# An encoder trunk's opening: transposes of x tiles in one row, or one tile at a time between the key/value products

## The reference

```python
proj = x @ w_in          # x (1, 512, 1024), w_in (1024, 512 + 2*128 + 2*512)
q, k, v, u = jnp.split(proj, [ATTN_WIDTH, ATTN_WIDTH + KV_WIDTH, ATTN_WIDTH + 2 * KV_WIDTH], axis=-1)
...
q = apply_rope(rms_norm(q, q_norm_g), cos, sin)
k = apply_rope(rms_norm(k, k_norm_g), cos, sin)
attn = block_attention(q, k, v)
conv = conformer_conv(u, dw_w, dw_b, conv_norm_g, conv_norm_b)
return jnp.concatenate([attn, conv], axis=-1) @ w_out
```

## Time and profile before

| what | value |
|---|---|
| time, median of 3 runs | 1415.85 us (1415.79 to 1416.1) |
| time of the profiled execution | 1417.29 us |
| span in the profile, first to last instruction | 1415.5 us |
| PE busy | 1389.9 us, 98% of the span |
| DVE, ACT, POOL busy | 656.0, 453.2, 117.6 us |
| mean granted clock of TensorE | 0.998 of full speed |

### The profile page before, as it was taken

One profiled execution on the slowest core, in us unless ns is written; L12 is line 12 of the kernel. 1 busy time (PEld: TensorE's weight loads), 2 busy tenths in 40 slices (PEclk: granted clock), 3 DMA queues, 4 the chain that ended last, 5 costly groups with the idle time before them and its releaser, 6 DMA issues.

```text
span 1415.5 us, 16267 instructions
## 1 busy us (share of the span) xinstructions
PE 1389.9 (98%) x6577; PEld 1157.4 (82%) x6577; DVE 656.0 (46%) x829; ACT 453.2 (32%) x601; POOL 117.6 (8%) x115
## 2 busy tenths in 40 slices
PE   7998999999999999999999999999999999999997
PEld 7876778988888888898888888888898888888886
DVE  5689966533333311266455554554264333332215
ACT  3448844332223211134232323333133232222111
POOL 5001012100000000060202020000030000000000
PEclk9999999999999999999999999999999999999999
DMA  6210002322332332222221212131323322333221
GB/s 215 73 49 31 30 31 62 118 89 90 100 106 89 119 111 97 89 75 90 86 93 59 89 59 89 60 119 62 112 65 97 111 89 89 112 107 108 90 89 60
DMA packets 84014, 124.14 MB, mean 88 GB/s; under 512 B 2688, under 2 KB 61312, under 8 KB 83968
## 3 DMA queue, kind: packets, MB, share of 16 engines
q1 hardware_dynamic: 83968, 123.49, 26.7%
HBM read 121.39 MB, written 2.10 MB: 87 GB/s over the span
## 4 chain that ended last, share of the span: by engine, by line
PE 91%; DVE 5%; ACT 1%; POOL 1%; issue 1%; DMA 0%; DVEq 0%; POOLq 0%; SPq 0%; ACTq 0%
PE ps L1228 23%; PE ps L1230 23%; PE ps L1229 23%; PE ps L1303 19%; DVE acc L868 1%; PE ps L1241 1%; POOL w_lo L375 1%; DVE w_lo L375 1%; DVE probT_lo L990 1%; ACT w_hi L371 1%; DVE neg_max L968 1%; PE ps L1444 0%; PE ps L1578 0%; DMA x_tok<-in_x 0%; DVE x_tok L1051 0%
## 5 line engine op out<-in xcount | busy, mean ns | idle before, releaser
L375 DVE TENSOR_TENSOR w_lo<-raw,w_hi 128x2048 fp32r<-128x2048 f32 x103 | 236.3, 2294 | 479.4 <-ACT w_hi L371 479.3
L1228 PE MATMUL ps<-xT_hi,w_hi 128*128 128x512 f32 (+1 forms) x992 | 366.7, 370 | 0.5 <-POOL w_lo L375 0.5
L1230 PE MATMUL ps<-xT_hi,w_lo 128*128 128x512 f32 (+1 forms) x992 | 365.6, 369 | 0.0
L1229 PE MATMUL ps<-xT_lo,w_hi 128*128 128x512 f32 (+1 forms) x992 | 365.5, 368 | 0.0
L371 ACT ACTIVATE w_hi<-raw 128x2048 fp32r<-128x2048 f32 x109 | 208.4, 1912 | 413.8 <-PE ps L1230 237.9
L1228 PEld LDWEIGHTS ps<-xT_hi,w_hi 128*128 128x128 f32 x992 | 187.0, 188 | 32.4 <-POOL w_lo L375 1.1
L1229 PEld LDWEIGHTS ps<-xT_lo,w_hi 128*128 128x128 f32 x992 | 187.0, 189 | 31.1
L1230 PEld LDWEIGHTS ps<-xT_hi,w_lo 128*128 128x128 f32 x992 | 187.0, 188 | 30.9
L1228 PE MATMUL ps<-w_hi,xT_hi 128*128 128x512 f32 (+1 forms) x320 | 121.3, 379 | 0.0
L1230 PE MATMUL ps<-w_hi,xT_lo 128*128 128x512 f32 (+1 forms) x320 | 121.1, 379 | 0.0
L1229 PE MATMUL ps<-w_lo,xT_hi 128*128 128x512 f32 (+1 forms) x320 | 121.1, 378 | 0.0
(11 more groups left out here) (161 smaller groups left out, 1611.3 us busy)
## 6 DMA issues: line engine op xcount, KB each, us to landing
raw<-in_l_w_in SPq DMA_DIRECT2D x31, 1024.0 KB, 5.2
raw<-in_l_ffn_w_gate SPq DMA_DIRECT2D x22, 1024.0 KB, 5.3
raw<-in_l_ffn_w_up SPq DMA_DIRECT2D x22, 1024.0 KB, 5.3
raw<-in_l_ffn_w_down SPq DMA_DIRECT2D x22, 1024.0 KB, 4.8
raw<-in_l_w_out SPq DMA_DIRECT2D x12, 1024.0 KB, 4.9
x_tok<-in_x SPq DMA_DIRECT2D x4, 512.0 KB, 7.5
out<-x_tok SPq DMA_DIRECT2D x8, 256.0 KB, 2.2
ln_gb<-in_l_ln_mix_g SPq DMA_DIRECT2D x2, 512.0 KB, 5.0
```

The costliest lines, as they stand in the source:

```text
L375: eng.tensor_tensor(w_lo[ch.s][:], raw[ch.s][:], f32(w_hi[ch.s][:]), ALU.subtract)\
L1228: nc.tensor.matmul(dst, a[0], b[0], start=start, stop=False)
L1229: nc.tensor.matmul(dst, a[0], b[1], start=False, stop=False)
L1230: return nc.tensor.matmul(dst, a[1], b[0], start=False, stop=stop)
```

## The change

The transposes of tile 0 still come first. Those of tile t + 1 are now issued inside `token_tiles`, ahead of the products of tile t, where the wait for the `xT_lo` of tile t also stands. The instructions are the same, in another order on PE; no other engine's text changes.

```diff
-            for t in range(TT):
-                turn_when_landed(t)
-            token_tiles([Chunk(C_KV)], SIDE_B, KD, 256, lambda t: pe.wait_ge(xT_lo_made, 2 * t + 2))
+            turn_when_landed(0)
+
+            def next_tile(t):
+
+                if t < TT - 1:
+                    turn_when_landed(t + 1)
+                pe.wait_ge(xT_lo_made, 2 * t + 2)
+
+            token_tiles([Chunk(C_KV)], SIDE_B, KD, 256, next_tile)
```

## The result

The changed kernel takes 1420.1 us in the median of 14 runs (1417.79 to 1420.7), the kernel before 1416.57 in 14 runs beside them (one of these took 6268.94 us; without it the median is 1416.54). The ratio is 1.002, with a 95% interval of 1.0014 to 1.0027: slower, by about 0.25% or 3.5 us, where 0.6 us was forecast and 1418.2 was the end of the range. The runs lie in two groups: 5 at 1417.8 to 1418.3 and 9 at 1420.0 to 1420.7, none between. The profiled run is one of the upper group, 1420.13 us with a span of 1418.3.

The account below looks back on a forecast made before the run. PE was taken to bound the kernel, busy 1389.9 of 1415.5 us. A new 1.19 us idle, less 0.58 because it falls where PE is slow, gave +0.6 us: 1416.45 us, own range 1416.2 to 1417.0, full range 1415.7 to 1418.2.

Parts of the forecast that it names:

- PE has no idle time to fill: From the first transpose at 7.8 us to 80 us, PE has no idle time that interleaving could fill.
- the new wait: After tile 0's transposes, at 9.53 us, PE waits for the first w_lo until 10.72: 1.19 us lost.
- The free change between transposes and products: Key/value products: switching between transposes and products costs nothing; at most 0.05 us allowed for each of six changes.
- the cover of chunk 1 and of the key work: Later splits and DVE's key work still finish before PE wants them; chunk 1's w_lo with 0.5 to 0.7 us left.
- d = 0: Opening: PE's rise to the high clock level stays at 13.7 us, so the 1.19 us idle costs 0.61 us.
- d/2: Opening: cost added to 0.61 us if the clock rise comes d later, since PE then does half the work.
- rival (a): Opening: the interrupted work delays the clock rise up to 16.6 us, costing up to +2.06 us, 1417.9; 24 in 100.
- my 2.06 us: Opening: upper sum, 0.61 + 1.45, if the low-level time is spent anew from 10.72 and PE rises at 16.6.
- the rest of the kernel is moved by PE's delay alone: After the opening all engines follow PE, and nothing there absorbs the 0.6 us delay.
- (b): Opening: PE stays at the low clock through the interleaving; up to +7.5 us, 1423.3; 5 in 100.
- (c): Opening: without a profiler the weights land earlier against x, so no idle time and 1415.85 us; 7 in 100.
- (c2): Opening: only products raise the clock, so the rise comes 1.75 us earlier, paying back 0.87: 1415.6; 2 in 100.

Follow-up runs that it names:

- e1: Changed kernel, but tiles 0 and 1 transposed ahead of the wait for the first w_lo, the others between the products; 1416.51 us, ratio 1.0.
- e2: Kernel before, all transposes in one row, with only the wait for the first w_lo put behind tile 0's transposes; 1418.27 us, ratio 1.0015.
- e9: Changed kernel with 14 unread identity transposes put into PE's 1.8 us pause before the last channel tile's first tap; 1418.24 us.
- e7: Kernel before, unchanged, run and profiled again; 1416.58 us in 8 runs.
- e3: Changed kernel with each key transpose at 42 us made twice, 8 more transposes (0.87 us of PE work); 1419.06 us.
- e4: Kernel before with each key transpose at 42 us made twice, 8 more transposes (0.87 us of PE work); 1418.23 us.
- e5: Kernel before with 28 unread identity transposes put on PE ahead of the first x tile; 1416.73 us.
- e10: Kernel before with 14 unread identity transposes put into PE's pause before the last channel tile's first tap; 1416.41 us, ratio 0.9999.
- e11: Kernel before with 28 identity transposes ahead of the first x tile and 14 in PE's pause at 140 us; 1415.27 us, ratio 0.9992.
- e6: Changed kernel with 28 unread identity transposes put on PE ahead of the first x tile; 1416.71 us.

## Why the prediction was wrong

**Right: PE has no idle time to fill.** The stretches said so, and e1 confirms it: interleaving without a wait changes nothing, within 0.1%.

**Right: the new wait.** 1.19 us forecast, 1.19 measured, at the forecast place; e1 and e2 show that it is the whole cause in the opening. The free change between transposes and products held too (0.12 and 0.87 us as before), as did the cover of chunk 1 and of the key work.

**Wrong: d = 0, the first failed step of two.** I took the rise to stay at 13.7 us, so that half the idle time would be given back. It came at 15.9, d = 2.2, or 2.3 counted from the first transpose, and the opening cost 1.55 us instead of 0.61 to 0.63. (The d/2 is a little too much, for products at the low level take 0.214 us and not twice 0.121: 0.61 + 0.43 x 2.2 = 1.56.) This is rival (a), which I gave 24 in 100. Over many runs the opening costs 1.8 us (e9 against before). Behind the choice stood the silent assumption that the moment of the rise is a property of the kernel, readable from one profile. e7 shows that it isn't: 2.9 and 6.0 us after the first transpose in the same kernel. The table has the first product at 16.45 to 17.96 with the opening of before (four profiles, and e1) and at 18.93 to 19.83 with that of the changed kernel (four). The Trainium skill's rule ("TensorE: Matmul & The Clock Gate", Part 1), that activity is judged in windows that run on freely, fits these runs, and I had quoted it without drawing a conclusion. What follows from the spread is argued, not shown: if the rise may come anywhere in a range before, then interrupting the work moves the whole range, and the mean delay of the rise is about the delay of the unbroken work, 2.9 us from 7.82 to 10.72. That gives my 2.06 us as the forecast; measured are 1.8. The same assumption let me take the 1.44 us between the profiled execution (1417.29) and the median for the profiler's. Each of the runs behind this document took 1.7 to 1.9 us more than its span, the profiled one among them, so it was the spread of the clock. The base was low for another reason besides: the 1415.85 is a median of three runs, and over 14 it is 1416.57. That is 0.7 us of the 3.65 between the 1416.45 that I named and the 1420.1 measured. And the range ended at 1418.2, though rival (a), at 24 in 100, was to reach +2.8 us, 1418.7.

**Wrong: "the rest of the kernel is moved by PE's delay alone."** This is the second failed step. The median of before and the opening's 1.8 us alone would make 1418.3, just past the end of the range; the falls took the median to 1420.1. In 12 of 22 runs, by the two profiles of the upper group, the shifted attention part met a fall of the clock that costs 1.5 us. Together, 1.8 for the opening and 12/22 x 1.5 for the falls are 2.6 us, where the means differ by 2.8. I had looked at pauses of up to 1.8 us and concluded from full clock in one profile that pauses leave it alone. The row that I cited for it, 40 nines, couldn't have shown a fall; that profile has none, but by its stretches, and e7's page with two falls shows 40 nines as well. Shown is that without the pause at 140 us the upper group is gone (e9), that the kernel before can have the fall too (e7), and that 0.87 us of shift changes how the runs fall out in both kernels (e3, e4). That the fall is commoner after the change because a late rise and a later attention part go together is argued from these, not shown: it would need the profiles of many runs.

**The rivals.** (b) is out: PE rose at 15.9 us while transposes and products alternated. (c) is out: the wait was there. (c2) is out as well: in e7 the rise came 2.9 us after the first transpose, with only transposes run, and in e5 before any product at all. The Trainium skill, same page, Part 4, has it that the full clock doesn't engage for transposes in TensorE's transpose mode. These float32 transposes against an identity bring it, 2.9 us after the first of them in e7; the rows call them MATMUL and don't show whether that mode is on.

## What to carry to other kernels

Before putting work behind a wait, ask what the wait was hidden by: here 24 transposes covered `w_lo`, and moving them uncovered 1.19 us although PE had no idle time to win. Where PE has pauses of 1 to 2 us, don't take the clock from one profile, nor from the digits of the page: look at several, by short stretches, and price both outcomes for every shift. A pause can be filled with transposes that nobody reads, here at no cost that showed (e9, e10), and two such fillings made e11, all of whose runs lie below all runs of before, by 1.2 us in the median. When times fall in two groups, compare the groups and not the medians.

## What the runs showed of the hardware

- The same kernel rises to the high clock level 2.9 or 6.0 us after its first transpose, and that alone moves everything behind by 1.5 us (1.76 less 0.25 for x).
- A low stretch lasts 3.4 us wherever a profile has one before the last microseconds, and costs 1.5 to 1.6 us where PE sets the pace (138 to 143 us) and 0 to 0.2 us where DVE does (102 to 110 us: e3, e6, e7, e10, e11).
- In the stretch ahead of the falls at 140 to 143 us PE had been busy for 1.41 of 3.40 us in the changed kernel, and for 1.64 in e7, with a pause of 1.8 us in it.
- The digits of the page don't show such a stretch: each of the 14 pages has 40 nines, with falls or without.
- The column of the granted clock shows a fall, but nothing of the low level before the first rise: there only the distance between starts tells.
- Products of 256 columns start 0.121 us apart at the high level and 0.214 at the low one, a ratio of 1.77; transposes 0.109 and 0.213, 1.96. What the low level costs depends on what runs in it.
